# Attention in a hybrid backbone step: tiles unrolled, a tile's output finished beside the next tile's heads

## The reference, cut to what matters

```
q = rms_norm(b_q) ; k = rms_norm(b_k)       # 8 query heads, 2 key/value heads, 64 wide
sample: q, k rotated; keys = 1024 own + 128 cached  -> s (1024 x 1152) for each head
prompt: keys = 128 own                              -> s (128 x 128) for each head
p = softmax(s * scale) ; o = p @ v ; o_att = o * silu(b_z)
```

## Time and profile before

| what | value |
|---|---|
| median of 3 runs | 4494.13 us (4482.1 to 4503.69) |
| profiled execution | 4498.94 us |
| its span in the trace | 4497.2 us |
| mean granted PE clock over the span | 0.934 of full speed |
| busy share of the span: PE, DVE, ACT, POOL | 88%, 48%, 23%, 13% |
| the attention's stretch, layer 1 and layer 2 | 282.4 us, 283.0 us |

### The profile page before, as it was taken

How to read it: one execution, slowest core, us unless ns; L and a number is a source line. 1 busy time by engine, 2 the same in 40 slices (tenths; PEclk the granted TensorE clock), 3 DMA queues, 4 the chain that set the end, 5 groups by cost and what they waited for, 6 DMA issues and landing times.

```text
span 4497.2 us, 70447 instructions
## 1 busy us (share of the span) xinstructions
PE 3937.8 (88%) x28051; PEld 3625.8 (81%) x28051; DVE 2171.6 (48%) x2549; ACT 1039.9 (23%) x1862; POOL 587.4 (13%) x711
## 2 busy tenths in 40 slices
PE   7999999995798887778989999999868889797688
PEld 4999999994577756768989999999847768397588
DVE  4521552106676775365464135411267766834553
ACT  3210110103445511130121011010234455103200
POOL 1000000013300141001010000000241001400100
PEclk8999999998899998888999999999989988898799
DMA  6222222227200552554332212222360024518432
GB/s 210 100 96 88 80 94 85 94 75 270 60 16 20 178 183 80 186 173 106 104 120 96 101 70 85 94 85 89 142 221 14 21 96 150 168 61 254 112 116 98
DMA packets 451084, 504.82 MB, mean 112 GB/s; under 512 B 82640, under 2 KB 386056, under 8 KB 447856
## 3 DMA queue, kind: packets, MB, share of 16 engines
q1 hardware_dynamic: 395416, 395.15, 26.7%
q0 software_dynamic: 33664, 94.85, 6.5%
q10 hardware_dynamic: 21728, 11.01, 0.9%
HBM read 333.91 MB, written 167.01 MB: 111 GB/s over the span
## 4 chain that ended last, share of the span: by engine, by line
PE 70%; issue 11%; DMA 6%; DVE 6%; DVEq 2%; SPq 2%; POOL 2%; ACT 1%; POOLq 0%; ACTq 0%
PE PSUM L698 15%; PE PSUM L700 15%; PE PSUM L699 15%; PE PSUM L1214 3%; PE PSUM L1235 3%; PE PSUM L1012 3%; PE PSUM L1361 2%; PE PSUM L1202 2%; PE PSUM L1203 2%; DMA xin<-proj_d 1%; SPq L936 1%; PE PSUM L1267 1%; PE PSUM L1266 1%; DMA qk_t<-proj_d 1%; PE PSUM L1320 1%
## 5 line engine op out<-in xcount | busy, mean ns | idle before, releaser
L698 PE MATMUL PSUM<-h_hi,w_hi 128*128 128x384 f32 x3360 | 1126.9, 335 | 9.0 <-DVEq L2202 9.0
L699 PE MATMUL PSUM<-h_lo,w_hi 128*128 128x384 f32 x3360 | 1124.7, 335 | 0.0
L700 PE MATMUL PSUM<-h_hi,w_lo 128*128 128x384 f32 x3360 | 1124.6, 335 | 0.0
L698 PEld LDWEIGHTS PSUM<-h_hi,w_hi 128*128 128x128 f32 x3360 | 632.5, 188 | 13.5 <-DVEq L2202 9.6
L699 PEld LDWEIGHTS PSUM<-h_lo,w_hi 128*128 128x128 f32 x3360 | 632.6, 188 | 0.0
L700 PEld LDWEIGHTS PSUM<-h_hi,w_lo 128*128 128x128 f32 x3360 | 632.4, 188 | 0.0
L682 DVE CAST w_hi<-w_raw 128x2048 fp32r<-128x2048 f32 (+1 forms) x104 | 118.9, 1143 | 748.1 <-PE PSUM L700 599.2
L1900 POOL DMA_DIRECT2D proj_d<-leave x140 | 81.1, 579 | 1689.1 <-ACT leave L1589 657.7
L698 PE MATMUL PSUM<-b_hi,w_hi 128*128 128x384 f32 x768 | 263.1, 343 | 42.2 <-DVEq L2512 15.0
L700 PE MATMUL PSUM<-b_hi,w_lo 128*128 128x384 f32 x768 | 261.4, 340 | 0.0
L699 PE MATMUL PSUM<-b_lo,w_hi 128*128 128x384 f32 x768 | 261.4, 340 | 0.0
(11 more groups left out here) (339 smaller groups left out, 6565.9 us busy)
## 6 DMA issues: line engine op xcount, KB each, us to landing
w_raw<-in_w_in SPq DMA_DIRECT2D x70, 1024.0 KB, 5.0
proj_d<-leave POOLq DMA_DIRECT2D x140, 512.0 KB, 2.9
g_t<-gdn_tile_d SPq DMA_DIRECT2D x72, 512.0 KB, 6.5
gdn_tile_d<-g_out SPq DMA_DIRECT2D x18, 1792.0 KB, 7.8
wide<-proj_d SPq DMA_DIRECT2D x48, 576.0 KB, 3.7
xs<-ssm_tok_d SPq DMA_DIRECT2D x36, 640.0 KB, 4.8
ssm_tok_d<-x_rest SPq DMA_DIRECT2D x36, 512.0 KB, 3.1
qk_t<-proj_d SPq DMA_DIRECT2D x36, 512.0 KB, 6.0
```

What stands on the lines that cost most here:

```text
L698: pe.matmul(dst, wh, x_hi[:, k, lo:hi], start=(k == 0), stop=False)
L699: pe.matmul(dst, wh, x_lo[:, k, lo:hi], start=False, stop=False)
L700: last = pe.matmul(dst, wl, x_hi[:, k, lo:hi], start=False, stop=(k == kt - 1))
```

## The change

The output of tile t is no longer finished behind its last head but beside heads 0 to 2 of tile t + 1. PE takes the values of the last head after the transposes of the next tile's head 0, turns `o_att` (now into bank 7) after the transposes of head 1, where the values of head 0 stood, and takes those at head 2, after a wait for `gated`. DVE scales before the row maximum of head 2 and gates after its copy for head 1. `at_v` is signalled once a tile. The loops of PE and ACT are written out. The queries are read from `q_stack`, and `q_now` with its copies is gone. The prompt's eight heads are taken together: one set of scores, one maximum, one subtraction on DVE into `prob[0]`, one exponent, eight transposes, two copies, row sums on DVE. The turning copies of `xy_out` go from ACT to GpSimd.

```diff
+        def slot(l, t, h):
+            return l * (NS * AH + 1) + t * AH + h
...
-                def scores(t, u, h):
+                def scores(t, h):
...
-                        pe.matmul(dst, q_now[u][:, h], k_hi[:, g, col:col + width], start=True, stop=False)
-                        last = pe.matmul(dst, q_now[u][:, h], k_lo[:, g, col:col + width], start=False, stop=True)
+                        pe.matmul(dst, q_stack[:, t, h], k_hi[:, g, col:col + width], start=True, stop=False)
+                        last = pe.matmul(dst, q_stack[:, t, h], k_lo[:, g, col:col + width], start=False, stop=True)
...
+                def turn_out(t):
+                    pe.wait_ge(o_norm, l * NT + t + 1)
+                    for k in range(4):
+                        last = pe.transpose(bank(7, P, k * P), o_att[:, 2 * k:2 * k + 2].rearrange("p h d -> p (h d)"), ident)
+                    last.then_inc(o_tr, 1)
+                scores(0, 0)
+                for t in range(NS):
                     for h in range(AH):
...
+                        if t or h:
+                            pe.wait_ge(at_c[1], slot(l, t, h))
                         if h + 1 < AH:
-                            scores(t, u, h + 1)
+                            scores(t, h + 1)
+                        elif t + 1 < NS:
+                            scores(t + 1, 0)
+                        else:
+                            prompt_scores()
+                        if t and h == 2:
                             pe.wait_ge(gated, nth(l, t, 0, 3))
...
+                            values(t, 0)
+                        turn(t, h)
+                        if t and h == 1:
+                            turn_out(t - 1)
+                        elif h:
+                            values(t, h - 1)
+                        elif t:
+                            values(t - 1, AH - 1)
+                values(NS - 1, AH - 1)
+                pe.wait_ge(at_e, slot(l, NS, 0) + 1)
+                for h in range(AH):
+                    last = pe.transpose(PSUM[:, 1536 + h * P:1536 + (h + 1) * P], prob[0][:, h * P:(h + 1) * P], ident)
...
+                turn_out(NS - 1)
...
+                pe.wait_ge(gated, nth(l, NS, 0, 3))
+                for h in range(AH):
+                    for half in HALVES:
+                        last = pe.matmul(bank(7, AD, h * AD)[half], prob_t[0][:, h, half], v_all[:, NS, h // 4 * AD:(h // 4 + 1) * AD], start=True, stop=True)
+                last.then_inc(at_v, 1)
+                turn_out(NS)
...
+                act.activation(prob[0][:, 0:1024], prob[0][:, 0:1024], ACT.Exp).then_inc(at_e, 1)
...
-                set_queries(0, 0, False)
-                set_queries(1, 1, False)
...
+                def flip_inverse(i):
...
+                    pool.wait_ge(u_done, l * 4 + i + 1)
...
+                    pool.tensor_copy(xy_out[rs, s, x].rearrange("p (j i) -> p j i", i=SOLVE), flip).then_inc(xy_done, 1)
...
+                def prompt_max():
...
+                    dve.tensor_reduce(row_max[:, 0], heads(PSUM[:, 0:1024]), AX_X, ALU.max, negate=True)
+                    dve.drain()
...
+                    dve.tensor_tensor(heads(prob[0][:, 0:1024]), heads(PSUM[:, 0:1024]), over(row_max[:, 0], P), ALU.add).then_inc(at_m, 1)
...
+                        if t and h == 1:
+                            out_scale(t - 1)
                         if h + 1 < AH:
-                            head_max(t, u, h + 1)
+                            head_max(t, h + 1)
+                        elif t + 1 < NS:
+                            head_max(t + 1, 0)
+                        else:
+                            prompt_max()
                         solve_slot(t * AH + h)
...
+                        if t and h == 1:
+                            out_gate(t - 1)
+                out_scale(NS - 1)
+                dve.wait_ge(at_e, slot(l, NS, 0) + 1)
+                dve.tensor_reduce(row_sum[:, 0], heads(prob[0][:, 0:1024]), AX_X, ALU.add)
...
+                out_gate(NS - 1)
+                dve.drain()
+                out_scale(NS)
+                out_gate(NS)
```

More of the change, by code:

```diff
@@ L1189, in _ @@
                 barrier(pe, l, 3)
-                def scores(t, u, h):
+                def scores(t, h):
                     g, s = h // 4, h % 2
[L1196 to L1200, removed]
+                    for col, width, at in ((0, 512, 0), (512, 512, 512), (NT * P, P, 1024)):
@@ L1204, in scores, with prompt_scores @@
                     last.then_inc(at_s, 1)
[L1206 to L1212, removed]
+                def prompt_scores():
+                    for h in range(AH):
+                        dst, g = PSUM[:, h * P:(h + 1) * P], h // 4
+                        pe.matmul(dst, q_stack[:, NS, h], k_hi[:, g, SAMPLE:T], start=True, stop=False)
+                        last = pe.matmul(dst, q_stack[:, NS, h], k_lo[:, g, SAMPLE:T], start=False, stop=True)
+                    last.then_inc(at_s, 1)
@@ new lines, in turn @@
+                def turn(t, h):
+                    m, s = slot(l, t, h), h % 2
+                    pe.wait_ge(at_e, m + 1)
+                    if t or h:
+                        pe.wait_ge(at_c[0], m)
+                    for j in range(9):
+                        dst = bank(6, P, j * P) if j < 4 else PSUM[:, 1536 * s + j * P:1536 * s + (j + 1) * P]
+                        last = pe.transpose(dst, prob[s][:, j * P:(j + 1) * P], ident)
+                        if j == 3:
+                            last.then_inc(at_t[0], 1)
+                    last.then_inc(at_t[1], 1)
@@ L1213, in values @@
+                def values(t, h):
+                    m, g, s = slot(l, t, h), h // 4, h % 2
+                    for c in range(2):
+                        pe.wait_ge(at_c[c], m + 1)
+                    sample_keys = (0, 1, 2, 3, 4, 5, 6, 7, NT)
+                    for j, kt in enumerate(sample_keys):
                         for half in HALVES:
                             last = pe.matmul(bank(7, AD, h * AD)[half], prob_t[s][:, j, half], v_all[:, kt, g * AD:(g + 1) * AD],
-                                             start=(j == 0), stop=(j == len(key_tiles) - 1))
@@ L1216, in values @@
-                    last.then_inc(at_v, 1)
-                def attn(t, u, key_tiles, first=False):
-                    n, nk = l * NT + t, len(key_tiles)
+                                             start=(j == 0), stop=(j == len(sample_keys) - 1))
+                    if h == AH - 1:
+                        last.then_inc(at_v, 1)
[4 more added lines that the diff above has]
+                    last.then_inc(o_tr, 1)
@@ L1228, in attn @@
[L1228 to L1231, removed]
-                            pe.wait_ge(gated, nth(l, t, 0, 3))
[L1233 to L1256, removed]
+                            scores(t, h + 1)
[3 more added lines that the diff above has]
+                            prompt_scores()
@@ new lines, in _ @@
+                pe.wait_ge(at_e, slot(l, NS, 0) + 1)
+                for h in range(AH):
+                    last = pe.transpose(PSUM[:, 1536 + h * P:1536 + (h + 1) * P], prob[0][:, h * P:(h + 1) * P], ident)
+                    if h in (3, 7):
+                        last.then_inc(at_t[h // 4], 1)
+                turn_out(NS - 1)
+                for c in range(2):
+                    pe.wait_ge(at_c[c], slot(l, NS, 0) + 1)
+                    pe.sem_inc(waits_held, 1)
+                pe.wait_ge(gated, nth(l, NS, 0, 3))
```

100 lines of the change are left out of this document (40 added, 60 removed).

## The result

The changed kernel takes 4434.66 us (median of 4 runs, 4423.3 to 4446.69), the kernel before in the same series 4489.19: a ratio of 0.9865, 95% interval 0.9838 to 0.9891. Two further series gave 0.9854 (0.9837 to 0.9870) and 0.9874 (0.9852 to 0.9896). On the 4494.13 of the forecast these are 4433, 4428 and 4437 us: 57 to 66 us less, where 47 were forecast. The sign and the order of size were right; the other ten to nineteen microseconds came from places that the prediction had mis-sized or not priced.

A forecast was written before the change was run, and what follows sets the result against it. A head is PE bound, with the gap at tile ends. Start 1.2, ends 14.9 and prompt 7.5 sum to 23.6 us a layer, 47.2 for two: from the median 4494.1 to 4447 us, range 4430 to 4470.

The forecast's parts named there:

- what the stage loses moves all that follows it: After attention: nothing is loaded ahead for later stages, so time saved in attention simply shifts the rest.
- slowed pace: Stage start: DVE's first solve product runs slowed beside GpSimd's second fill, ending about 1191.0 instead of 1192.27; 1.2 us saved.
- The ends: Seven tile ends a layer: 26.9 us before, 12.0 after, 14.9 saved, of which 5.2 is PE's loop jump.
- the prompt: Eight prompt heads taken together: 22.1 us before, end at 14.2 after, 7.9 saved, taken as 7.5 (bounds 5.5 to 9).
- the 4.52 us of the earlier trace: Stage start, kernel before: time of DVE's first solve product beside GpSimd's second fill, read as a product slowed 2.3 times.
- the 1.93 that I had set against it: Stage start, kernel before: time of a later, like solve product of DVE, taken as the undisturbed length.
- The jump: PE's loop jump at one tile end a layer, that end at 8.3 us; straight code saves 5.2 of it.
- median step: DVE's solve step in a head, 0.26 to 0.96 us, median 0.76; with it PE stalls 0.8 for the gate.
- 0.2 + 2s: Cost of a new tile end, s being DVE's solve step: 1.7 us in place of 3.1.
- only moved: Rival at tile ends: the gate wait costs PE the old 3.1 us; 19.6 given back, 4466 us; chance 0.14.
- z_b's single buffer: Prompt's end: the gate factor's load, issued after the gate before, lands at 13.5 us, so the end is at 14.2.
- the cover of 2.3: Tile 7: some 2.3 us until DVE's next solve product hide each GpSimd turning copy; cost 0 to 0.4, taken as nothing.

The follow-up runs named there:

- the two padded kernels: Counting instructions added on DVE after its attention stage: 32 in the kernel before, ratio to it 0.9992; 17 in the changed kernel, ratio to the kernel before 0.9903.
- the run with the fills moved: The changed kernel with GpSimd's row fills moved behind its turning copies; ratio 0.9875 to the kernel before.

## Why the forecast was right in kind and short in size

Two steps failed. The prediction put the rest of the layer at nothing ("what the stage loses moves all that follows it"), and the two scans came out 13 us shorter. And it let DVE's product and GpSimd's fill share at a "slowed pace", a start 1.2 us shorter, where the start is set by who comes first and came out 1.0 or 6.1 shorter. The ends and the prompt were right in mechanism and off by 1.9 and 0.9 a layer, in opposite directions.

**Start: they do not share.** In the stage of layer 1:

```profile
1186.19 5.35 POOL L1985 TENSOR_SCALAR s_row<-head_of 128x2048 fp32r<-128x2048 f32 x1
1186.30 3.63 DVE L2352 TENSOR_TENSOR bk_p<-bk_p,beta_p 128x96 f32<-128x96 f32 x1
...
1190.00 1.23 DVE L2373 TENSOR_TENSOR u_sol<-u_raw,bk_p 128x1024 f32<-128x1024 f32 x1
```

DVE came 0.11 us behind the fill, and a product of 96 columns that takes 0.26 took 3.63. Then a product of 1,024 columns ran at full rate beside the same fill. So the 4.52 us of the earlier trace rows were about 3.3 of blocking and 1.23 of work; the 1.93 that I had set against it belongs to the second block, whose product takes 1.91 to 2.04 with no hold. That this case saves 1.0 us, near the 1.2 of the forecast, is luck. In the changed kernel run again DVE got there between the fills:

```profile
1182.42 5.38 POOL L1985 TENSOR_SCALAR s_row<-head_of 128x2048 fp32r<-128x2048 f32 x1 [0.19 <-issue]
...
1187.11 0.26 DVE L2352 TENSOR_TENSOR bk_p<-bk_p,beta_p 128x96 f32<-128x96 f32 x1
...
1187.68 1.23 DVE L2373 TENSOR_TENSOR u_sol<-u_raw,bk_p 128x1024 f32<-128x1024 f32 x1 [0.32 <-issue]
1187.78 1.28 POOL L1986 CAST s_col<-cst 128x128 fp32r<-128x128 f32 x1
...
1190.78 3.68 DVE L2373 TENSOR_TENSOR u_sol<-u_raw,bk_p 128x1024 f32<-128x1024 f32 x1
```

DVE's first product of 1,024 columns was 0.10 ahead here, and GpSimd's 0.28 copy waited (1.28). The second product, behind the second fill (at 1189.03), took 3.68. That the first holder keeps the port and the other stands still is the rule of the Trainium skill (SBUF — State Buffer, "SBUF: two separate sides") that the prediction had weighed and set aside. The trace agrees with it on who blocks. On how long, it nearly agrees in the run with the fills moved, where the multiplication was released 5.2 us into a 5.35 us fill, but not here, where both products were released 3.5 us into the fill.

What decides the race is PE's clock in the first heads, since DVE's chain begins behind PE's scores. Windows of 5 us, from 1 us behind the first load, both layers of the changed kernel:

```profile
1181.10:1186.10 5.00, 4.34 (x17) 3.72 (x17) 3.58 (x4) 1.31 (x2) 5.00 (x2) 0.51 0.19 56
3354.58:3359.58 5.00, 2.72 (x18) 2.13 (x17) 4.12 (x6) 1.90 (x3) 5.00 (x2) 1.00 0.19 52
```

The same of the second layer with the fills on ACT, where POOL is idle:

```profile
3352.09:3357.09 5.00, 4.34 (x17) 3.68 (x17) 3.51 (x4) 1.31 (x2) 0.00 (x0) 0.50 0.21 56
```

DVE's 96-column product in that stage, 6.27 us behind its first load (3351.09), from the timeline:

```profile
3357.36 0.26 DVE L2357 TENSOR_TENSOR bk_p<-bk_p,beta_p 128x96 f32<-128x96 f32 x1
```

And the window of the first layer of the kernel before:

```profile
1180.44:1185.44 5.00, 4.06 (x12) 3.25 (x12) 2.11 (x2) 1.02 (x1) 4.81 (x4) 0.66 0.18 52
```

A granted 1.00 is the level of 2.4 GHz, 0.50 that of 1.2. Of the 14 stages in kernels of the new kind with fills at the start, the eight at 1.00 all won the race (start 31.8 to 31.9 us), the six at 0.50 to 0.71 all lost it (36.6 to 36.9). Counted from the stage's first load, the second fill can start at 6.09; DVE's 96-column product started at 5.15 to 5.17 where the clock read 1.00. At 0.50 and with no fill to hold it, it started at 6.27, and in the six lost races at 6.20 to 6.64. Without the fills the start is 30.2 at 1.00 and 32.5 at 0.50. So the lower clock itself costs 2.3, the fills 1.7 in the good case and 4.3 in the bad. In the kernels of the old kind, with PE waiting for GpSimd's copy, all eight stages read 0.50 to 0.67. Why the clock differs between executions of one kernel was not found.

**Ends: the structure held, the size was 2.2 short.** The jump was priced right (8.3 against 3.35 alone). The new ends measure 1.61, 2.05, 2.31, 2.35, 2.21, 1.86 and 1.79, growing to tile 4, 14.2 together for a forecast 12.0. PE's wait for the gate was 1.30 at tile 4, where I had put 0.8 for a median step. With each tile's own steps in place of the median, 0.2 + 2s gives 1.36, 1.82, 2.06, 2.12, 1.96 and 1.61 for the first six, and the measured ends lie 0.23 to 0.25 above: PE starts 0.98 and not 0.75 behind the gate (a counting instruction stands between; that it is the cause was not tried). The seventh end carries two products and two updates, 1.22 in all, instead of two steps. The seven old ends were 27.2, not 26.9. Saved 13.0, not 14.9. The rival "only moved" fell: no end reaches 3.1.

**Prompt: 0.9 better than taken.** The working itself gave 7.9; I took off 0.4 for a lower clock. Saved 8.4, in the main since the sixteen products came 0.11 apart (1.84 us, not 2.2). z_b's single buffer ended it, as worked out.

**GpSimd's turning copies: right.** 2.0 us each, inside the cover of 2.3.

**The scan: never priced.** The prediction held that all behind attention merely moves. The scans are 13 us shorter in both layers together, and the two padded kernels show that the place of the loop in DVE's code does it. Not all of it reaches the whole time: scan and what lies behind it, both layers, took 2447.4 us in the mean of the two profiles of the kernel before and 2441.0 in the three of the changed one, 6 us less. That the longer issue (0.28 to 0.56 instead of 0.18) is the fetch of the next block of DVE's code, whose boundary the change moved out of the loop, fits the Trainium skill (Runtime: NRT & Kernel Launch, "Instruction fetch mechanics": code is loaded in blocks, and a branch to code that is no longer held costs a fetch); no row shows the fetch itself, so this is argued, not shown.

The sum as measured, a layer: start 1.0 or 6.1, ends 13.0, prompt 8.4, and for the scan 6.6 at most, 3 by what reaches the end. For two layers that is 51 to 58 us with both starts bad and 61 to 68 with both good; the three ratios lie at 57 to 66.

## What to carry to other kernels

Where two engines race for a port, look in the trace for who starts first and by how much: DVE's product 0.11 us behind a fill lost 3.4 us, a sum of DVE in the scan, 0.03 us behind GpSimd's product, lost 1.7, and an edit that shifts one of them, or only the code's length, changes the winner far away from itself. Before comparing a slowed instruction with "the like one", check that both have the same layout when undisturbed. Take work off the engine whose fills hold DVE, to a place where its new engine waits anyway: put into ACT's waits, the fills delayed nobody at the start (they met no two-input product of DVE there, so the runs do not show what such a meeting would cost). And one copy moved off the engine that sets the wait gave 0.57 us at each of 14 ends. Price the stretches that an edit does not touch by profiling them, not by taking them as fixed.

## What the hardware showed that I had not expected

- A GpSimd fill recorded at 5.35 us let a two-input product of DVE go 3.5 us after its own start, and a one-input multiplication of eight columns 5.2 us after it, yet a one-input instruction of 96 columns begun 4.5 us into such a fill (1185.08 in layer 1 of the changed kernel) took only 0.31. Which property makes the difference was not tried.
- In a scan whose loop runs on DVE, an issue gap of 0.28 to 0.56 instead of 0.18 us at a fixed place of the code made three of the loop's four passes 1.84 us longer (the second 16.5 instead of 14.7), through the port, not by its own length.
- The clock at the start of a stage read 1.00 or about 0.5 to 0.7 in executions of one and the same kernel.
